# A six-layer float32 network on one core: the start, the norms, the tap copies, the mLSTM gates and the last norm rewritten

## The reference, cut to what matters

```
first_block, 2 layers:
    h = rms_norm(x, norm1_w); proj = h @ w_in       # z | xbc | dt | q | k | v
    xbc = silu(conv7(xbc)); y_ssm = ssd(...) ; y_attn = windowed attention
    x = x + mixed @ w_out ; x = x + (silu(conv3(g)) * u) @ w_down
second_block, 4 layers:
    x = layer_norm(ALPHA * x + (1 + gate1) * branch(h), g, b)
    h = x * (1 + scale2) + shift2
    x = layer_norm(ALPHA * x + (1 + gate2) * conv_ffn(h), g, b)
branch 0: u = glu(h @ w); u = conv31(u); silu(layer_norm(u)) @ w
branch 2: hc = head_norm(mlstm(...)); ((hc * norm_g + skip * xc) * silu(z)) @ w
layer_norm(x): mu = mean(x); (x - mu) * rsqrt(mean((x - mu)^2) + eps) * g + b
```

## Time and profile before

| what | value |
|---|---|
| runs | 2558.65, 2556.23, 2558.38 us (median 2558.38) |
| the profiled execution | 2558.1 us |
| its span, first to last instruction or DMA | 2556.4 us |
| TensorE busy | 2514.4 us, 98% of the span |
| VectorE, ScalarE, GpSimd busy | 51%, 22%, 6% |
| mean granted TensorE clock | 0.996 of full speed |
| DMA | 457.65 MB, 179 GB/s mean |

### The profile page before, as it was taken

How to read it: one execution, slowest core, us unless ns; L and a number is a source line. 1 busy time by engine, 2 the same in 40 slices (tenths; PEclk the granted TensorE clock), 3 DMA queues, 4 the chain that set the end, 5 groups by cost and what they waited for, 6 DMA issues and landing times.

```text
span 2556.4 us, 35348 instructions
## 1 busy us (share of the span) xinstructions
PE 2514.4 (98%) x14807; PEld 2182.0 (85%) x14807; DVE 1314.1 (51%) x3085; ACT 556.4 (22%) x1090; POOL 164.9 (6%) x266
## 2 busy tenths in 40 slices
PE   8999999999999999999999999999999999999998
PEld 7878888987888897988898888898788889888887
DVE  6652774565277546499453479652524332324422
ACT  2451100144110023211041211023402111532101
POOL 2000110000021000011000121030000000000000
PEclk9999999999999999999999999999999999999999
DMA  6835885473489645688453588642244444424441
GB/s 199 234 100 183 288 290 194 137 197 97 130 316 313 210 148 137 212 308 285 152 165 115 183 282 301 206 145 87 95 132 137 159 141 140 132 99 148 148 152 62
DMA packets 402777, 457.65 MB, mean 179 GB/s; under 512 B 50159, under 2 KB 374824, under 8 KB 402620
## 3 DMA queue, kind: packets, MB, share of 16 engines
q1 hardware_dynamic: 369170, 339.95, 42.4%
q0 software_dynamic: 29648, 111.68, 12.1%
q10 hardware_dynamic: 3802, 3.78, 0.6%
HBM read 453.34 MB, written 2.02 MB: 178 GB/s over the span
## 4 chain that ended last, share of the span: by engine, by line
PE 90%; DVE 5%; DMA 2%; ACT 2%; issue 1%; ACTq 0%; POOL 0%; DVEq 0%; POOLq 0%
PE job_bank L859 65%; PE job_bank L914 9%; PE mix_bank L914 3%; PE job_bank L1258 3%; DVE sb_arena L2442 1%; DVE sb_arena L2416 1%; DMA sb_t<-row_scratch 1%; PE mix_bank L1205 1%; ACT sb_h L1752 1%; PE job_bank L1233 1%; PE mix_bank L1169 1%; PE mix_bank L1506 1%; PE mix_bank L1219 1%; PE mix_bank L890 1%; DVE sb_rstd L2347 0%
## 5 line engine op out<-in xcount | busy, mean ns | idle before, releaser
L859 PE MATMUL job_bank<-sb_h,sb_ring 128*128 128x256 f32 x5920 | 1302.4, 380 | 0.0
L859 PEld LDWEIGHTS job_bank<-sb_h,sb_ring 128*128 128x128 f32 x5920 | 1116.5, 190 | 169.6 <-issue 17.2
L859 PE MATMUL job_bank<-sb_arena,sb_ring 128*128 128x256 f32 x1840 | 401.1, 380 | 0.0
L859 PEld LDWEIGHTS job_bank<-sb_arena,sb_ring 128*128 128x128 f32 x1840 | 348.7, 190 | 51.2 <-issue 3.5
L2416 DVE SCALAR_TENSOR_TENSOR sb_arena<-sb_arena,sb_par 128x256 f32<-128x256 f32 x722 | 333.7, 502 | 13.3
L2442 DVE SCALAR_TENSOR_TENSOR sb_arena<-sb_arena,sb_c_act 128x256 f32<-128x256 f32 x672 | 326.0, 485 | 24.0
L1717 ACT ACTIVATE sb_arena<-job_bank 128x512 f32<-128x512 f32 x178 | 106.3, 597 | 1034.1 <-PE job_bank L859 979.8
L914 PE MATMUL job_bank<-sb_h,sb_ring 128*128 128x128 f32 x1600 | 188.0, 276 | 8.3 <-ACT sb_h L1752 5.6
L914 PEld LDWEIGHTS job_bank<-sb_h,sb_ring 128*128 128x128 f32 x1600 | 182.0, 192 | 12.9 <-issue 7.0
L1721 ACT ACTIVATE sb_t<-sb_x 128x512 f32<-128x512 f32 (+1 forms) x57 | 32.0, 561 | 520.2 <-DVE sb_x L2284 270.3
L805 POOL DMA_DIRECT2D sb_arena<-in_ada_w x96 | 84.9, 885 | 857.7 <-DVE sb_arena L2442 535.0
(11 more groups left out here) (428 smaller groups left out, 1746.4 us busy)
## 6 DMA issues: line engine op xcount, KB each, us to landing
sb_arena<-in_ada_w POOLq DMA_DIRECT2D x96, 1024.0 KB, 7.7
sb_ring<-in_ffn_w_up SPq DMA_DIRECT2D x88, 1024.0 KB, 5.1
sb_ring<-in_w_up SPq DMA_DIRECT2D x44, 1024.0 KB, 7.4
sb_ring<-in_ffn_w_down SPq DMA_DIRECT2D x32, 1024.0 KB, 5.2
sb_ring<-in_w_in SPq DMA_DIRECT2D x24, 1024.0 KB, 5.7
sb_ring<-in_w_down SPq DMA_DIRECT2D x16, 1024.0 KB, 6.2
sb_ring<-in_hg_w_in SPq DMA_DIRECT2D x16, 1024.0 KB, 5.5
sb_ring<-in_ml_w_up SPq DMA_DIRECT2D x16, 1024.0 KB, 5.5
```

Of the source, the lines that this page charges most:

```text
L859: mm = pe.matmul(o, st, mv, start=(k0 + k == 0 and t == 0), stop=(k0 + k == kn - 1), skip_group_check=True)
```

## The change

Seven edits.

1. Start: the second token half's square sum goes to VectorE (one multiply-and-sum instruction). TensorE turns raw x at once into M0 to M3; ScalarE copies it to `x`. The reciprocal root is put on the diagonal of two 128x128 tiles by VectorE, and a product with ones spreads it over all partitions; VectorE makes `h` from `x`, the column of norm1_w and that. That column alone is waited for first; the other early rows are turned after x. The later 16 transposes of x and their four copies go.
2. The dt job runs after the fourth xbc job, before the last two; VectorE and ScalarE do its rows between the convolutions; POOL's second broadcast waits for the convolutions.
3. `centre_half` subtracts the mean from four tiles while ScalarE takes the root, then multiplies two tiles, two tiles, then subtracts and multiplies the other four. The squares for the second half are put inside the eight tiles of `h`; `whole_sums` comes two products after `tail_sums`, not four, in norms with a mean.
4. Long convolution: no DRAM copy; 16 small DMAs from `cc_u` to `cc_u4` per pair of tiles, issued by ScalarE; of the last pair SyncE issues eight.
5. mLSTM: head i's gate product moves to the next head, between VectorE's copy of the sums and its use of the statistics; `fill` counts change; ScalarE does `head_deviation(3)` before it reads z job 5.
6. Last norm by tokens: TensorE turns raw x (before the norm) back while the last job runs, ScalarE copies and squares with sums, VectorE sums, and mean, variance, g and b are applied with tokens on partitions. POOL loads g and b as rows over all partitions. The output leaves in four DMAs of 256 KB.
7. `lbs` moves to another buffer; `ones` is set first.

```diff
+        def spread_pair(eng, i, groups):
+
+            first = max(2 * i, CC_DVE_TILES)
+            n = 2 * i + 2 - first
+            at = first - CC_DVE_TILES
+            for g in groups:
+                for r in range(4):
+                    eng.dma_start(cc_u4[32 * r:32 * r + 32, at:at + n, g, :],
+                                  cc_u[32 * g:32 * g + 32, first:first + n, r:r + CC_U4]).then_inc(s.cu4_in[i - 1], 16)
...
+                    read_out(sp, plan["pw1"][-1])
+                    spread_pair(sp, KD // 2 - 1, (0, 1))
+                    sp.wait_ge(s.cu4_in[-1], 256)
...
-                return {at: lambda: tail_sums(norm, jobs_, ns, half), at + 4: lambda: whole_sums(norm, half)}
+                gap = 2 if norm == "mean" else 4
+                return {at: lambda: tail_sums(norm, jobs_, ns, half), at + gap: lambda: whole_sums(norm, half)}
...
+            def last_project(jobs_, rhs, ready):
+
+                for i, job in enumerate(jobs_[:3]):
+                    run(job, rhs, ready if i == 0 else None)
+                    if i:
+                        read_out(pe, jobs_[i - 1])
+                        mm = turn_final((2 * i - 2, 2 * i - 1), range(NT))
+                mm.then_inc(s.fin_turned, 1)
+                half_pass(jobs_[3], rhs, 0).then_inc(s.half_done, 1)
+                read_out(pe, jobs_[2])
+                turn_final((4, 5), range(NT)).then_inc(s.fin_turned, 1)
+
+                def first_tail():
+
+                    read_out(pe, jobs_[3])
+                    turn_final((6, 7), (0,)).then_inc(s.fin_turned, 1)
+
+                half_pass(jobs_[3], rhs, 1, bank=M[2], hooks={8: first_tail})
+                pe.wait_ge(s.tail_x, due(s.tail_x))
+                turn_final((6, 7), (1,)).then_inc(s.fin_turned, 1)
...
+            turn_x(0)
+            turn_x(1)
+            pe.wait_ge(s.rstd_tok, 3)
+            for j in range(NT):
+                mm = pe.matmul(L[2][:, j * P:(j + 1) * P], ones[:, :], rs_diag[:, j, :], start=True, stop=True)
+            mm.then_inc(s.x_turned, 1)
+            turn_x(2)
+            turn_x(3)
...
-            fill(beside, 16)
+            fill(beside, 17)
             for i in range(ML_HEADS):
                 ml_values(i)
                 if i + 1 < ML_HEADS:
                     ml_scores(i + 1)
-                fill(beside, 5)
+                fill(beside, 5 if i + 1 < ML_HEADS else 7)
                 head_sums(i)
                 fill(beside, 2)
                 head_stats(i)
-                fill(beside, 4)
+                fill(beside, 5)
...
+            def modulate_half(n, half, groups, after={}):
 
                 c = slice(half * P, (half + 1) * P)
                 for k in range(KD):
-                    if k % group == 0:
+                    if k in after:
+                        after[k]()
+                    if k in groups:
                         act.wait_ge(s.xc_ready, due(s.xc_ready))
                     act.activation(h[:, k, c], x[:, k, c], ACT.Identity, scale=lnp[:, n % 2, 0, k:k + 1],
                                    bias=lnp[:, n % 2, 1, k:k + 1]).then_inc(s.h_ready, 1)
...
+            act.wait_ge(s.x_in[0], 16)
+            step(act.activation(t1[:, 0:4, :].rearrange("p k t -> p (k t)"), x_tok[:, 0, :], ACT.Square,
+                                accum_out=ms_tok[:, 0:1]))
+            settle()
+            act.wait_ge(s.ms_tok, 1)
             act.activation(ms_tok, ms_tok, ACT.Sqrt, scale=1.0 / D, bias=eps[:, 0:1]).then_inc(s.ms_tok, 1)
+            act.wait_ge(s.x_turned, 1)
+            act.activation(first_w, L[1][:, 0:KD], ACT.Copy).then_inc(s.x_ready, 1)
+            for b, turned in enumerate((2, 3, 5, 6)):
+                act.wait_ge(s.x_turned, turned)
+                act.activation(x[:, 2 * b:2 * b + 2, :], pair(M[b]), ACT.Copy).then_inc(s.x_ready, 1)
...
-                act.dma_start(u_dram[first:first + n, :, :].rearrange("m q w -> q m w"), cc_u[:, first:first + n, :])\
-                   .then_inc(s.cu_out, 16)
-                act.wait_ge(s.cu_out, 16 * i)
-                at = first - CC_DVE_TILES
-                for r in range(4):
-                    src = bass.AP(u_dram.tensor, first * P * CC_U + r, [[CC_U, 32], [32 * CC_U, 4 * n], [1, CC_U4]])
-                    act.dma_start(cc_u4[32 * r:32 * r + 32, at:at + n, :, :].rearrange("p n g t -> p (n g) t"), src)\
-                       .then_inc(s.cu4_in, 16)
+                spread_pair(act, i, groups)
...
+            def final_keep(ks, j):
+
+                bank, _ = fin_bank(ks[0], j)
+                w = slice(ks[0] * P, (ks[-1] + 1) * P)
+                act.activation(x_tok[:, j, w], bank[:, 0:len(ks) * P], ACT.Copy).then_inc(s.fin_act, 1)
...
+                def centre(k, n):
+                    step(vec.tensor_tensor(v[:, k:k + n, c], v[:, k:k + n, c], along(red[:, lo], n), ALU.subtract))
+
+                def scale(k, n):
+                    vec.tensor_tensor(v[:, k:k + n, c], v[:, k:k + n, c], along(rstd[:, lo], n), ALU.mult)\
+                       .then_inc(s.xc_ready, 1)
+                    due(s.xc_ready)
+                centre(0, 4)
                 vec.wait_ge(s.std_ready, due(s.std_ready))
                 step(vec.reciprocal(rstd[:, lo], std[:, c]))
                 settle()
-                step(vec.scalar_tensor_tensor(out=red[:, hi], in0=red[:, lo], scalar=-1.0, in1=rstd[:, lo],
-                                              op0=ALU.mult, op1=ALU.mult))
-
-                def along(w):
-                    return w.unsqueeze(1).to_broadcast([P, 4, P])
-                for k in (0, 4):
-                    step(vec.tensor_tensor(v[:, k:k + 4, c], v[:, k:k + 4, c], along(rstd[:, lo]), ALU.mult))
-                    settle()
-                    vec.tensor_tensor(v[:, k:k + 4, c], v[:, k:k + 4, c], along(red[:, hi]), ALU.add)\
-                       .then_inc(s.xc_ready, 1)
-                    due(s.xc_ready)
+                scale(0, 2)
+                scale(2, 2)
+                centre(4, 4)
+                settle()
+                scale(4, 4)
...
+                    sums((6, 7), j)
+                    settle()
+                    step(vec.tensor_scalar(fin_v[:, 8, c], fin_v[:, 2, c], fin_v[:, 6, c], -1.0 / D, ALU.add, ALU.mult))
+                    settle()
+                    step(vec.tensor_tensor(fin_v[:, 9, c], fin_v[:, 8, c], fin_v[:, 8, c], ALU.mult))
+                    vec.wait_ge(s.fin_act, 10 + 2 * j)
+                    step(vec.tensor_scalar(fin_v[:, 12, c], fin_v[:, 5, c], fin_v[:, 7, c], 1.0 / D, ALU.add, ALU.mult))
+                    settle()
+                    vec.tensor_tensor(fin_v[:, 10, c], fin_v[:, 12, c], fin_v[:, 9, c], ALU.subtract)\
+                       .then_inc(s.var_ready, 1)
+                    due(s.var_ready)
+                    for q in range(2):
+                        w = slice(q * D // 2, (q + 1) * D // 2)
+                        step(vec.scalar_tensor_tensor(out=x_tok[:, j, w], in0=x_tok[:, j, w], scalar=fin_v[:, 8, c],
+                                                      in1=fin_g[:, w], op0=ALU.add, op1=ALU.mult))
+                    vec.wait_ge(s.std_ready, due(s.std_ready))
+                    step(vec.reciprocal(fin_v[:, 13, c], fin_v[:, 11, c]))
+                    settle()
+                    for q in range(2):
+                        w = slice(q * D // 2, (q + 1) * D // 2)
+                        vec.scalar_tensor_tensor(out=x_tok[:, j, w], in0=x_tok[:, j, w], scalar=fin_v[:, 13, c],
+                                                 in1=fin_b[:, w], op0=ALU.mult, op1=ALU.add).then_inc(s.fin_read, 1)
...
+            vec.wait_ge(s.x_in[1], 16)
+            vec.tensor_tensor_reduce(out=t1[:, 4:8, :].rearrange("p k t -> p (k t)"), in0=x_tok[:, 1, :],
+                                     in1=x_tok[:, 1, :], scale=1.0, scalar=0.0, op0=ALU.mult, op1=ALU.add,
+                                     accum_out=ms_tok[:, 1:2]).then_inc(s.ms_tok, 1)
+            vec.wait_ge(s.ms_tok, 2)
             vec.reciprocal(rs_tok, ms_tok).then_inc(s.rstd_tok, 1)
             own(s.rstd_tok, 1)
-            vec.tensor_scalar(h_tok[:, 0, :], x_tok[:, 0, :], rs_tok[:, 0:1], None, ALU.mult).then_inc(s.hn_ready[0], 1)
+            vec.wait_ge(s.const_done, 2)
+            for j in range(NT):
+                vec.tensor_scalar(rs_diag[:, j, :], ident[:, :], rs_tok[:, j:j + 1], None, ALU.mult)\
+                   .then_inc(s.rstd_tok, 1)
...
+                vec.wait_ge(s.x_turned, 4)
+                step(vec.tensor_copy(rstd[:, 0:T], L[2][:, 0:T]))
+                settle()
+                for k in range(KD):
+                    vec.wait_ge(s.x_ready, 2 + k // 2)
+                    vec.scalar_tensor_tensor(out=h[:, k, :], in0=x[:, k, :], scalar=first_w[:, k:k + 1],
+                                             in1=rstd[:, 0:T], op0=ALU.mult, op1=ALU.mult).then_inc(s.h_ready, 1)
...
+            def gate_head(m0, n):
+
+                v = ml_q[:, m0:m0 + n, :]
```

(6 more changed lines are left out.)

324 lines of the change are left out of this document (169 added, 155 removed).

## The result

| | before | after |
|---|---|---|
| median, us (4 runs each) | 2558.52 | 2521.82 (2520.59 to 2522.39) |
| profiled span, us | 2556.4 | 2520.0 |
| first product of the first job, us | 14.59 | 12.10 |
| last weight product to end of span, us | 15.4 | 8.1 |

The ratio is 0.9853, 95% interval 0.984 to 0.9865: 36.7 us less. 29 were predicted, and the time lies just under the range. The direction and each place were right, the size was not.

What follows compares the result with a forecast made beforehand. TensorE, busy 98% of the span, was taken as the bound. Gains of 3.0 + 1.8 + 6.5 + 2.9 + 1.7 + 1.2 + 3.4 + 2.9 + 5.8 = 29.2 us off 2558.1 gave 2529 us, range 2522 to 2541.

Steps and rivals of the forecast that it cites:

- the reciprocal begins about 0.8 us sooner: Start: with the second square on VectorE, the reciprocal begins near 7.6 us; part of the 3.0 us gain.
- rival B: Start: the lower clock holds into the first job, gain 1.4 instead of 3.0 us, 2530 to 2531 us; chance 0.08.
- of 5.6 + 1.9 = 7.5 us I take 6.5; bounds 3.5 and 7.5: Norms: gain 6.5 us from TensorE's waits for `h` (5.6) and for squares (1.9).
- the squares would be late next: Norms with two jobs halved: squares before the sixth tile of `h` take 0.4 to 0.8 us, which the lead just covers.
- eight are 3.8 us: Long convolution: issuing eight direct tap copies takes 3.8 us, at a median of 0.47 each.
- all in by 991.5 to 994.2: Long convolution: the last direct copies land by then, before TensorE wants them at 994.6, so the 2.9 us wait goes.
- The 1.2 for `h`: Behind the long convolution: the 2.64 us wait for `h` shortens by 1.2 us, bounds 0 to 2.6.
- 3.4, and half of the 5.82 us at the lower clock, 2.9. Bounds: ... 6.3 at best: mLSTM heads: moving the gate product removes a 3.4 us wait and 2.9 us of lower clock; lower bound 3.4.
- the span ends 3.4 us after: End: the span ends 3.4 us after the last store is issued; part of the 5.8 us gain.
- Rival D: Whole kernel: each part gains its upper bound, 34.0 us in all, 2524 us; chance 0.06.
- A: Whole kernel: the next late thing takes the place of removed waits, gain only 13.4 us, 2545 us; chance 0.11.
- C: Long convolution: small DMAs of one queue finish one after another, so the kernel is slower, 2598 us; chance 0.03.

Runs made afterwards that it cites:

- experiment 10: The kernel after with the dt job and its rows back behind the xbc jobs, on all engines, in both layers: 2521.54 us, 0.3 less.
- experiment 8: The kernel after, unchanged, measured once more for the spread between executions: 2522.78 us, span 2521.0.
- experiment 4: The kernel after with the long convolution's tap copies through DRAM, all from ScalarE's queue, as before: 2526.87 us, 5.0 more.
- experiments 1 and 2: The kernel after with the norms as before, 2533.31 us; then only their order, squares' place or sums' distance as before: lead lost 5.0, 0.0, 1.4 us.

## Why the prediction was short

The direction, each place and the order of the parts were right; the terms of the norms, the mLSTM heads and the end were too small by 3.8, 2.3 and 1.6 us. The step that failed in the first two is one: the sum books a stall of TensorE at the idle time that the view of waits lists, and takes that for its upper bound.

**Start.** 3.0 predicted, 2.5 in this pair of executions. The step "the reciprocal begins about 0.8 us sooner" failed: 8.41 became 8.02, because the second tile of x lands at 6.3 and its square takes 1.23. And rival B was no rival but a spread. Its chance of 0.08 was wrong: in ten of the twelve executions in the experiments the first unit ended 0.5 to 1.7 us later than in the profiled one (in two of these 0.3 and 0.7 of it is a later first job), so the profiled one was the lucky case. With the half pace lasting to 12.0 us in one execution of a program and to 14.8 in another, the trace agrees with what the prediction cites from the Trainium skill, "TensorE: Matmul & The Clock Gate", section on the clock gate: the point of release differs from execution to execution.

**Transposes of x, dt.** 1.8 against 1.7, and 0 against 0 (experiment 10). Right.

**Norms.** The failed step is "of 5.6 + 1.9 = 7.5 us I take 6.5; bounds 3.5 and 7.5". It measured 10.3, outside the bounds, for one reason: idle time in the waits counts from the drawn end of a product, and the stall counts from where the next product could have started, and the first record behind it is slow as well. From the lengths of the records (0.28 us, 0.112 us apart) 2.1 of the 2.8 us could have been read before. The worry that the squares would be late next was empty.

**Convolution.** 5.8 against 5.2. The failed step is "eight are 3.8 us", and with it "all in by 991.5 to 994.2". ScalarE issues the direct copies 0.62 us apart, which makes 5.0, and its last eight took 6.5 us (980.25 to 986.78), because one issue in each queue was long while both were issuing: 2.24 us on SyncE, 1.68 on ScalarE. The last copy was in at 990.2, which is 995.0 in the times of before (the kernel after is 4.9 us ahead there), 0.8 beyond my latest. In experiment 8 the two long issues are 1.58 and 1.04 us, the last copy is in at 993.2 of before, inside my bounds, and nothing waits. The eleven executions with direct copies agree: the 0.5 us wait for squares stands where SyncE's long issue took 2.2 us (three executions), 0.3 and 0.1 of it at 1.97 and 1.86, none at 1.74 or less. What makes the issue long stays open. Without these stalls the part gives 6.5 to 6.8 us, more than the 5.8, since the sum had left out the overlap and this wait of before:

```profile
PE mix_bank L1327 <- DMA sb_arena<-gated_scratch: 0.5, 1, 0.5
```

The lower clock was worth 1.7 here, and 2.9 in experiment 4. The 1.2 for `h` came (2.64 to 1.38).

**mLSTM.** The failed step is "3.4, and half of the 5.82 us at the lower clock, 2.9. Bounds: ... 6.3 at best". 8.6 in this pair, 8.0 when put back. The two terms booked measured 3.4 and 2.7 to 2.9. Left out were four small waits (1.2) that went with the same edit (by its counts of products or by ScalarE's order, which was not tried apart), and again the overlap, six times: the sixth is a stall of 0.22 us in front of the first head's values, of which only 0.06 is idle.

**End.** 5.8 against 7.4, outside my bound of 7.0. The chain of waits of the kernel after, last pieces [against rows 12, 13]:

```profile
2503.89 8.05 PE mix_bank L947 x72
...
2511.97 0.62 DVE sb_x L2378 x2
...
2514.71 1.33 DVE sb_arena L2466 x2
...
2516.14 0.75 DVE sb_arena L2473
2516.90 0.66 DVEq L368
```

The last store is issued at 2517.6: 5.65 us behind the last product where I had 6.0, and the span ends 2.4 after it where I had 3.4. The step that failed is "the span ends 3.4 us after": I carried the landing of the second of two crowded 512 KB stores over to a 256 KB store that follows another of 256 KB. That is 1.0 of the 1.6; the rest is in the small operations and the transposes in front, booked at 6.2 in all.

Rival D, "more goes than I book", was the case that came, and even its sum was too low by 2.4 us: the norms, the mLSTM heads and the end passed its bounds by 2.8, 2.3 and 0.4, the first two since the bounds were built on the same idle times; the start and the convolution stayed below them. A, C and the case on the slower side did not come.

## What to carry to other kernels

Where products overlap in the record, price a stall of TensorE from start to start: take the pace of the products ahead of it, not the idle time that the waits list, and count the stalls, since each hides about the same amount (here 0.16 us of overlap and up to 0.10 in the slow record behind it, for products that follow each other every 0.112 us; 15 stalls listed at 7.5 us cost 10.3). Edits to one join share their slack: undone one by one these three cost 6.3 us, together 10.3, so none of them may be judged by taking it out alone. And here each stall of 2.8 to 3.4 us in the middle was followed by a lower clock that cost another 1.4 us in one kernel and 3 in another.

## What was unexpected of the hardware

- The granted clock reads 1.00 in every stretch of the first 15 us, while the products come at half the pace (6 and 11 in 2.10 us, experiment 8), since the clock record has no entry before the release. At the start the pace, and not PEclk, tells.
- The length of the 0.50 stretch is not set by the stall before it: 5.8, 5.3 and 2.9 us behind the same 3.4 us, and 3.3, 5.9 and 2.9 us behind 2.9, 3.0 and 2.8. Behind the stall of 2.64 us at 1012.05, and behind 2.2 in experiments 1 and 2, none was seen.
- Issuing a copy from SBUF to SBUF cost ScalarE 0.62 us, and one to or from DRAM 0.36 to 0.47; 48 of 36 to 71 KB from two queues landed in 1.9 to 5.5 us. While both queues were issuing, one issue in each took far longer, 1.4 to 2.2 us on SyncE and 1.0 to 1.7 on ScalarE, over the eleven executions with direct copies.
